# An encoder layer on one core: split halves of W_in kept in DRAM, all conv taps on VectorE, the sample gather issued ahead of the weight subtracts

## The reference

```
h    = rmsnorm(x) * g
q, k, v, cv, cg = split(h @ w_in)            # w_in: 1024 x 1792
A    = attention(rope(rms(q)), rope(rms(k)), v)            # 8 heads on 2, width 64
C    = silu(layernorm(depthwise_conv31(cv * sigmoid(cg)) + b))
x    = x + concat(rms(A), rms(C)) @ w_out
h    = rmsnorm(x);  aff = softmax(h @ w_router)
for each of 16 experts: the top 128 tokens (prompt) and top 64 (sample) by aff:
    y[rows] += gate * (silu(h[rows] @ w_gate) * (h[rows] @ w_up)) @ w_down
```

## Time and profile before

| | |
|---|---|
| median of three runs | 2681.26 us |
| the profiled execution, its own time | 2678.6 us |
| its span, first to last instruction | 2676.7 us |
| busy in the span: TensorE, VectorE, ScalarE, GpSimd | 2555.7, 1852.6, 1393.3, 385.6 us |
| DMA | 477.37 MB, mean 178 GB/s |
| projection of the prompt, of the sample | to 197, to 277 us |
| turning of q and k, attention | 282 to 314, to 628 us |
| output projection and choice, experts | to 876, to 2677 us |

### The profile page before, as it was taken

How to read it: one execution, slowest core, us unless ns; L and a number is a source line. 1 busy time by engine, 2 the same in 40 slices (tenths; PEclk the granted TensorE clock), 3 DMA queues, 4 the chain that set the end, 5 groups by cost and what they waited for, 6 DMA issues and landing times.

```text
span 2676.7 us, 40151 instructions
## 1 busy us (share of the span) xinstructions
PE 2555.7 (95%) x15982; PEld 2349.6 (88%) x15982; DVE 1852.6 (69%) x2177; ACT 1393.3 (52%) x1687; POOL 385.6 (14%) x329
## 2 busy tenths in 40 slices
PE   8989799996995999999999999999999999999997
PEld 8878689985884989999899998999989999899996
DVE  6788899985348567666676666766667666676674
ACT  4233556667222556556565564655656556465563
POOL 3635890000001001001010010100101001010010
PEclk9999999998997999999999999999999999999999
DMA  4122000002323767777687786777868778677773
GB/s 155 44 65 82 1 1 1 1 1 104 111 95 127 233 227 248 225 254 247 223 255 232 242 252 229 248 226 251 249 223 256 231 241 254 229 248 224 244 243 111
DMA packets 348093, 477.37 MB, mean 178 GB/s; under 512 B 10000, under 2 KB 301200, under 8 KB 347792
## 3 DMA queue, kind: packets, MB, share of 16 engines
q1 hardware_dynamic: 340880, 449.74, 51.6%
q0 software_dynamic: 7040, 25.17, 3.8%
HBM read 449.71 MB, written 25.17 MB: 177 GB/s over the span
## 4 chain that ended last, share of the span: by engine, by line
PE 89%; DVE 5%; ACT 3%; issue 1%; POOL 1%; DMA 1%; SPq 0%; ACTq 0%; POOLq 0%; DVEq 0%
PE psum L1592 30%; PE psum L1594 14%; PE psum L1325 8%; PE psum L1326 8%; PE psum L1327 8%; PE psum L1461 5%; PE psum L1614 4%; PE psum L1615 4%; PE psum L1448 2%; PE psum L1436 2%; DVE conv L893 1%; ACT probs L666 1%; PE psum L1577 0%; PE psum L1527 0%; DVE wi_lo L920 0%
## 5 line engine op out<-in xcount | busy, mean ns | idle before, releaser
L1232 DVE TENSOR_TENSOR w_lo<-raw,w_hi 128x2048 fp32r<-128x2048 f32 x384 | 880.0, 2292 | 494.9 <-ACT w_hi L775 493.0
L1592 PE MATMUL psum<-xgT,w_hi 128*128 128x384 f32 x4096 | 1169.0, 360 | 2.4 <-issue 2.4
L1594 PE MATMUL psum<-xgT,w_lo 128*128 128x192 f32 x4096 | 1026.6, 251 | 0.0
L775 ACT CAST w_hi<-raw 128x2048 fp32r<-128x2048 f32 x384 | 733.7, 1911 | 333.0 <-PE psum L1615 333.0
L1594 PEld LDWEIGHTS psum<-xgT,w_lo 128*128 128x128 f32 x4096 | 784.0, 191 | 0.6
L1592 PEld LDWEIGHTS psum<-xgT,w_hi 128*128 128x128 f32 x4096 | 770.5, 188 | 3.5 <-issue 2.8
L549 POOL DMA_INDIRECT out_dram<-o_p,put_p x16 | 25.7, 1605 | 1542.6 <-ACT o_s L822 1471.7
L893 DVE SCALAR_TENSOR_TENSOR conv<-conv,colp 128x1024 f32<-128x1024 f32 (+1 forms) x210 | 236.4, 1126 | 4.0
L1325 PE MATMUL psum<-w_hi,hid_st 128*128 128x512 f32 x512 | 212.9, 416 | 0.0
L1326 PE MATMUL psum<-w_lo,hid_st 128*128 128x512 f32 x512 | 202.5, 396 | 0.0
L1327 PE MATMUL psum<-w_hi,hid_st 128*128 128x512 f32 x512 | 202.4, 395 | 0.0
(11 more groups left out here) (216 smaller groups left out, 3531.8 us busy)
## 6 DMA issues: line engine op xcount, KB each, us to landing
raw<-in_w_gate_dram SPq DMA_DIRECT2D x128, 1024.0 KB, 5.3
raw<-in_w_up_dram SPq DMA_DIRECT2D x128, 1024.0 KB
raw<-in_w_down_dram SPq DMA_DIRECT2D x128, 1024.0 KB, 4.9
wi_raw<-in_w_in_dram SPq DMA_DIRECT2D x56, 256.0 KB, 3.8
out_dram<-x SPq DMA_DIRECT2D x12, 512.0 KB, 2.6
h_rows<-h SPq DMA_DIRECT2D x12, 512.0 KB, 2.9
wo_raw<-in_w_out_dram SPq DMA_DIRECT2D x8, 512.0 KB, 7.3
xres<-in_x_prompt_dram SPq DMA_DIRECT2D x8, 512.0 KB, 4.1
```

The source lines that it names most:

```text
L775: act.copy(w_hi[:, j % SPLIT_SLOTS, :], raw[:, j % RAW_SLOTS, :]).then_inc(e_hi, 1)
L1232: dve.tensor_tensor(w_lo[:, j % SPLIT_SLOTS, :], raw[:, j % RAW_SLOTS, :], w_hi[:, j % SPLIT_SLOTS, :].bitcast(F32), ALU.subtract).then_in ...
L1592: pe.matmul(bank[:, 0:2 * CAP], w_hi[:, slot, w0:w0 + P], xgT[:, half, k, :], start=(k == 0), stop=False, skip_group_check=True)
L1594: last = pe.matmul(bank[:, 0:CAP], w_lo[:, slot, w0:w0 + P], xgT[:, half, k, 0:CAP], start=False, stop=(k == KD - 1), skip_group_check=True)
```

## The change

*W_in's halves.* After each prompt chunk's split, SP writes the halves to a DRAM buffer `wi_kept` (4 writes of 512 KB per chunk, `keep_wi`). For the sample it loads both halves of a chunk whole, two loads of 1 MB (`load_kept`), as soon as TensorE has multiplied the chunk two before. No raw load, cast or subtract remains for the sample; TensorE waits on the load. ScalarE's cast into a slot waits until the slot's earlier halves are written out.

*Conv taps.* The taps of the sample's block 0 join `TAPS` on VectorE; GpSimd has none. Gated blocks of the sample run 6, token steps of its token chunks 0 and 1 run 2. The conv transposes of prompt tiles wait for the prompt's taps alone, and up to 14 units of the sample may still run one tap each.

*The sample gather.* GpSimd waits for two row arrays in place of three, issues, does a small copy, and signals `asked`. VectorE does the prompt's low half first, waits for `asked`, subtracts chunks 0 and 1, then the sample's low half, then chunk 2 onward.

```diff
+    wi_kept = nc.dram_tensor("wi_kept", [CHUNKS, 2, P, KD * CCOLS], F32).ap()
...
-        TAPS = [(0, c, k) for c in range(NC_CONV) for k in range(CONV_K)] + [(1, c, k) for c in (1, 2, 3) for k in range(CONV_K)]
-        POOL_TAPS = [(1, 0, k) for k in range(CONV_K)]
+        TAPS = [(0, c, k) for c in range(NC_CONV) for k in range(CONV_K)] + [(1, c, k) for c in range(NC_CONV) for k in range(CONV_K)]
+        PROMPT_TAPS = NC_CONV * CONV_K
...
+            def keep_wi(place, halves=(0, 1)):
+                for hf in halves:
+                    ks = slice(hf * KD // 2, (hf + 1) * KD // 2)
+                    sp.wait_ge(wi_l, 2 * place + hf + 1)
+                    for x, half in enumerate((wi_hi, wi_lo)):
+                        sp.dma_start(wi_kept[place, x].rearrange("p (k c) -> p k c", k=KD)[:, ks, :], half[:, place % 2, ks, :].bitcast(F32)
+                                     ).then_inc(kept[place % 2], 16)
+            def load_kept(place):
+                n = CHUNKS + place
+                if place < 2:
+                    sp.wait_ge(kept[0], 64 * (3 + place))
+                    sp.wait_ge(kept[1], 64 * 3)
+                wi_multiplied(sp, n - 2)
+                for x, half in enumerate((wi_hi, wi_lo)):
+                    sp.dma_start(half[:, n % 2, :, :].bitcast(F32), wi_kept[place, x].rearrange("p (k c) -> p k c", k=KD)
+                                 ).then_inc(wi_back[n % 2], 16)
...
             for c in range(1, CHUNKS):
-                load_wi(0, c)
+                load_wi(c)
+                keep_wi(c - 1)
             load_x(ROT_TILES)
             load_x(ROT_TILES + 1)
-            load_wi(1, 0)
+            keep_wi(CHUNKS - 1)
+            load_kept(0)
             for t in range(ROT_TILES + 2, TILES):
                 load_x(t)
             for c in range(1, CHUNKS):
-                load_wi(1, c)
+                load_kept(c)
...
-            pool.wait_ge(sample_rows, 3)
+            pool.wait_ge(sample_rows, 2)
             y_stored(pool)
             pool.sem_inc(dma_turn, 1)
             pool.indirect_dma_start(xg_s[:, :], None, h_rows, bass.IndirectOffsetOnAxis(ap=rows_sg[:, 0:1], axis=0)
                                     ).then_inc(gathered_s, 16)
+            pool.tensor_copy(cur_sg[:, :], rows_sg[:, 0:1]).then_inc(asked, 1)
+            pool.wait_ge(asked, 1)
+            pool.wait_ge(sample_rows, 3)
...
                 if n >= 2:
                     wi_multiplied(act, n - 2)
+                    act.wait_ge(kept[n % 2], 64 * (n // 2))
...
-                    if place + 1 < CHUNKS:
-                        split_wi(g, place + 1)
+                    if g == 0 and place + 1 < CHUNKS:
+                        split_wi(place + 1)
...
-                            if (g, c) == (0, 2) and t == nt - 1:
-                                split_wi(1, 0)
...
-                    conv_run(6 if g == 0 else 4)
+                    conv_run(6)
...
-                    conv_run(1)
+                    conv_run(1 if g == 0 or c == 2 else 2)
...
                     conv_run(3 - (u % 4 == 0) if sample_next else 2 - u % 2)
+                elif u < PROMPT_UNITS + 2 * ROT_TILES - 2:
+                    conv_run(1)
                 else:
                     conv_run(len(TAPS))
...
-            for j in range(SPLIT_SLOTS):
+            dve.wait_ge(xg_ph, 1)
+            prompt_low(0)
+            dve.wait_ge(asked, 1)
+            for j in range(2):
                 step(0, j)
-            gathered_low(0, 0)
-            for j in range(SPLIT_SLOTS, TURN):
+            dve.wait_ge(xg_h, 1)
+            sample_low().then_inc(xg_l, 1)
+            for j in range(2, TURN):
                 step(0, j)
...
-                    if ch:
+                    if g == 1:
+                        pe.wait_ge(wi_back[ch % 2], 32 * (place // 2 + 1))
+                    elif ch:
                         pe.wait_ge(wi_l, 2 * ch + 2)
...
-                pe.wait_ge(conv_tap, len(TAPS))
-                pe.wait_ge(pool_tap, len(POOL_TAPS))
+                pe.wait_ge(conv_tap, PROMPT_TAPS if g == 0 else len(TAPS))
```

More of the change, by code:

```diff
@@ L141, in encoder_layer_kernel @@
                 sq = in_region(ra, "sq", [P, CCOLS], F32)
-                tapped = in_region(ra, "tapped", [P, N_SAMPLE], F32)
                 hstat = in_region(ra, "hstat", [P, 2, 3, 4], F32)
@@ L227, in encoder_layer_kernel @@
         wi_h = sem("wi_h"); wi_l = sem("wi_l")
+        kept = [sem(f"kept{i}") for i in range(2)]; wi_back = [sem(f"wi_back{i}") for i in range(2)]
         pr_glu = sem("pr_glu"); glu_sig = sem("glu_sig"); glu_u = sem("glu_u")
@@ L230, in encoder_layer_kernel @@
         t_rstd = sem("t_rstd"); t_norm = sem("t_norm"); rope_a = sem("rope_a"); rope_b = sem("rope_b"); rope_c = sem("rope_c")
-        v_ok = sem("v_ok"); conv_tap = sem("conv_tap"); pool_tap = sem("pool_tap"); pool_mul = sem("pool_mul")
+        v_ok = sem("v_ok"); conv_tap = sem("conv_tap");
         qk_hi = sem("qk_hi"); qk_lo = sem("qk_lo"); qk_T = sem("qk_T"); q_st_ok = sem("q_st_ok"); k_st_ok = sem("k_st_ok")
@@ L252, in encoder_layer_kernel @@
         e_hi = sem("e_hi"); e_lo = sem("e_lo"); e_used = sem("e_used")
-        dma_turn = sem("dma_turn"); cur_ok = sem("cur_ok"); cur_s_ok = sem("cur_s_ok"); put_ok = sem("put_ok"); gathered = sem("gathered"); gathered_s = sem("gathered_s"); xg_T = sem("xg_T"); xg_h = sem("xg_h"); xg_l = sem("xg_l")
+        dma_turn = sem("dma_turn"); cur_ok = sem("cur_ok"); cur_s_ok = sem("cur_s_ok"); asked = sem("asked"); put_ok = sem("put_ok"); gathered = sem("gathered"); gathered_s = sem("gathered_s"); xg_T = sem("xg_T"); xg_h = sem("xg_h"); xg_l = sem("xg_l")
         g_low = sem("g_low"); g_sum = sem("g_sum"); g_act = sem("g_act"); u_low = sem("u_low"); u_sum = sem("u_sum")
@@ L371, in load_x, with load_wi @@
                 sp.dma_start(x_place(t), x_rows(t)).then_inc(x_in[t % ROT_TILES], 16)
-            def load_wi(g, place, halves=(0, 1)):
-                n = CHUNKS * g + place
-                kind, c = ORDER[place]
+            def load_wi(n, halves=(0, 1)):
+                kind, c = ORDER[n]
                 for hf in halves:
@@ L392, in _ @@
             sp.dma_start(colp[:, :], cols).then_inc(consts_in, 16)
-            load_wi(0, 0, (0,))
+            load_wi(0, (0,))
             load_x(2)
-            load_wi(0, 0, (1,))
+            load_wi(0, (1,))
             for t in range(3, ROT_TILES):
@@ L500, in _ @@
                 pool.tensor_tensor(dst, qn[:, n % 2, 0:w], q_turn[:, 0:w], ALU.add).then_inc(rope_c, 1)
[L502 to L513, removed]
             pool.wait_ge(prompt_rows, 1)
@@ L585, in split_x, with split_wi @@
                 act.copy(hT_hi[:, :, i * P:(i + 1) * P], x_transposed(t)).then_inc(hT_h, 1)
-            def split_wi(g, place, halves=(0, 1)):
-                n = CHUNKS * g + place
+            def split_wi(n, halves=(0, 1)):
                 if n >= 2:
                     wi_multiplied(act, n - 2)
+                    act.wait_ge(kept[n % 2], 64 * (n // 2))
                 for hf in halves:
@@ L631, in _ @@
                         if t < 2:
-                            split_wi(0, 0, (t,))
+                            split_wi(0, (t,))
                 for place, (kind, c) in enumerate(ORDER):
-                    if place + 1 < CHUNKS:
-                        split_wi(g, place + 1)
+                    if g == 0 and place + 1 < CHUNKS:
+                        split_wi(place + 1)
                     if kind == "glu":
@@ L887, in conv_run @@
                         dve.wait_ge(glu_u, glu_no[g, c, GROUPS[g][2] // 512 - 1] + 1)
-                        if g == 1:
-                            dve.wait_ge(pool_tap, len(POOL_TAPS))
                         dve.tensor_scalar(out, u, tap, colp[:, COL_BIAS + c:COL_BIAS + c + 1], ALU.mult, ALU.add
@@ L1255, in hid_low, with prompt_low, sample_low @@
                                   ALU.subtract).then_inc(h_lo, 1)
-            def gathered_low(e, half):
[L1258 to L1265, removed]
+            def prompt_low(half):
+                return dve.tensor_tensor(xgT[:, half, :, CAP:CAP + CAP_P], gathered_prompt(),
+                                         xgT[:, half, :, 0:CAP_P].bitcast(F32), ALU.subtract)
+            def sample_low():
+                return dve.tensor_tensor(xgT[:, :, :, CAP + CAP_P:2 * CAP], gathered_sample(),
+                                         xgT[:, :, :, CAP_P:CAP].bitcast(F32), ALU.subtract)
+            def gathered_low(e, half):
+                dve.wait_ge(xg_h, e + 1)
+                last = prompt_low(half)
                 if half == 0:
-                    last = dve.tensor_tensor(xgT[:, :, :, CAP + CAP_P:2 * CAP], gathered_sample(),
-                                             xgT[:, :, :, CAP_P:CAP].bitcast(F32), ALU.subtract)
+                    last = sample_low()
                 last.then_inc(xg_l, 1)
```

## The result

The changed kernel takes 2666.08 us (median of 5 runs, 2664.14 to 2666.31), the kernel before 2681.09 us beside it (5 runs, 2678.01 to 2682.63): a ratio of 0.9943, interval 0.9930 to 0.9956. Forecast were 2668.8 us and a range of 2663 to 2675. Its profiled execution took 2666.08 us with a span of 2664.3 us; against the profiled execution of before (2678.6 and 2676.7) that is 12.5 us, the sum forecast. The medians lie 15.0 us apart because the profiled execution of before is one of the quick ones of its kernel, that of after its median. What makes some executions of before quicker than others is not known.

The account below looks back on a forecast made before the run. TensorE was taken to bound the kernel, with 89% of the chain of waits. Terms −8, −3, +3.5 and −5 sum to −12.5 us, from 2681.26 to 2668.8 us, range 2663 to 2675.

Parts of the forecast that it names:

- the sum forecast: Whole kernel: −8 − 3 + 3.5 − 5 = −12.5 us against the profiled execution.
- prompt attention: Prompt attention's 64 units: without GpSimd's taps all run at 3.61 us, 231 in place of 238.8 us; −8 us.
- The argument from pace and pair of taps: Prompt attention: units 3.95 us beside GpSimd's taps, 3.61 after; two VectorE taps 3.50 against 2.60 us.
- Turning q and k: Stage from 282 to 314 us: small splits that TensorE awaits get shorter without GpSimd's taps; −3 us, bounds 0 and −4.
- the three shorter stretches: Turning of q and k: three stretches of about 0.3 to 0.4 us, counted beside two long ones.
- The split read as running alone: Turning of q and k: a small split taking 0.41 us alone, against 1.48 beside GpSimd's taps.
- Sample projection: Sample's projection: subtracts go, 16 taps come, VectorE ends at 284.0 in place of 280.5; +3.5 us, bounds +0.3 and +9.
- the mean of the window: Sample's projection: each VectorE tap costs 1.40 us, from 27 taps taking 37.82 us.
- The rival of taps contended throughout: Sample's projection: VectorE late, +9 in place of +3.5 us, so 2674.3 us; chance 0.12.
- Queue and kept halves: SP's writes and sample loads: costed at nothing, each later kept pair covered by one TensorE chunk of 11.3 us.
- Start of the experts: Sample gather: issues unheld by VectorE's subtracts, first expert matmul at 871.4 in place of 876.44; −5 us, bounds −6 and −0.2.

Follow-up runs that it names:

- The late pairs: Changed kernel with a 2 MB DRAM-to-DRAM copy queued ahead of each kept pair but the first: 2677.82 us.
- The run with one subtract: Changed kernel with one VectorE subtract of 2048 columns between the prompt's low half and the wait for GpSimd's issue: 2668.93 us.
- the run with copies: Changed kernel with three VectorE copies of 2048 columns between the prompt's low half and the wait for GpSimd's issue: 2666.06 us.
- both edits: Changed kernel with no tap behind the sample's last gated block and attention's row scaling on ScalarE instead of VectorE: 2654.71 us, 0.9912.

## Why the prediction was right

*What bounds it, and prompt attention* (−8): −8.3. Five kernels separate the causes: with GpSimd's taps the 64 units take 238.8 and 238.7 us, without them 230.2, 230.5 and 230.6, whatever else is changed. The argument from pace and pair of taps was the right one. What it took for VectorE's pace is TensorE's as much: VectorE relieved by 14.7 us gave 2.8.

*Turning q and k* (−3): −2.1. The two long splits of 1.48 us became 0.42, which is 2.1 us and the whole of what the stage gained; the three shorter stretches that the term also counted went too, and seem to have been covered, which no run tests. The run without GpSimd's taps gave −1.7. The split read as running alone lay beside a GpSimd multiply (292.86 to 294.47 us), the long one beside an add (291.01 to 292.75); the runs without these taps have the same 0.42.

*Sample projection* (+3.5, an end of VectorE at 284.0): 284.54, and the first q 4.1 us later. Of this 0.8 us came from ahead of the sample's projection: the changed kernel was at 191.67 where before was at 190.89, so TensorE began at 195.64 and not by 195. That isn't shown to be the queue or the kept writes, which were costed at nothing: over all kernels here this point lies between 190.58 and 192.38, with kept halves alone at 190.89, without GpSimd's taps and with no such writes at 192.38. Less this, +3.3. But the stage moves by nearly as much from run to run: without GpSimd's taps the first q came 3.0 us later than before, by the same code. The taps cost what the mean of the window said: in the groups of VectorE from 209 to 284.6 us 42 of them take 59.5 us, 1.42 each, against 1.40, and behind the first gated block VectorE waited for no other, as reckoned. The rival of taps contended throughout did not come.

*Queue and kept halves* (0): no wait; pairs of 1 MB loads land in 4.8 and 6.9 us, inside the 11.3 us. The late pairs show the cover that was reckoned with (11.1 us for a pair that took 14.5), and more only behind a late one.

*Start of the experts* (−5): the issue 0.96 us, landing after 4.3, and the stage 5.7 us shorter; undone it costs 5.2. The forecast took 5.2 us for the landing, as of the prompt's gather; the 0.9 us less is why the stage gained more than reckoned. As to "SBUF — State Buffer", section "Who interferes with whom" of the Trainium skill: by its inferred clause these subtracts would not hold descriptor generation. Here they held the issue, 6.6 us against 0.96 in two kernels that differ in the start of the experts alone. The same section says that the order of issue decides who blocks. The run with one subtract, where GpSimd was first, agrees; the run with copies, where GpSimd was first by as much and the issue took 1.75 us, does not.

*What was not in the sum*: the last sample units gave back about 1 us (9.57 us from the 93rd to the last maximum against 8.50, at a mean granted clock of 0.82 against 1.00), and the expert stage gained 1.0. They cancel, and the second is within what this stage moves: 1798.4 to 1800.6 us in all kernels here but the one with both edits.

So the sum of 12.5 was right by terms of which none is off by more than 1 us. That it met the spans to 0.1 us is luck: the terms missed by 0.3 to 0.9 us to either side. The difference between the medians is 2.5 us more only because of where the profiled execution of before lies among its runs.

## What to carry to other kernels

Before moving work onto an engine, look at what stands behind it there: the taps paid on VectorE only because the splits that TensorE waited for had been taken away, and either edit tried alone would have been judged far from its worth in the pair. Where an engine looks gapless beside another that looks gapless, take some work off one before forecasting from it. And cost a late transfer with its buffers: with two of them a late load shelters the next.

## What the runs showed of the hardware

Taps on GpSimd slow work on VectorE: two VectorE taps took 3.50 us beside GpSimd's and 2.60 alone. Of the small splits, both of 1.48 us began during a GpSimd add; those that began during a multiply took 0.41 or 0.42 us. VectorE subtracts running back to back stretched the issue of an indirect DMA on GpSimd to 6.6 us in place of 0.96, a single one under way to 2.24 us, and one that began after it didn't; a subtract with one input in PSUM (855.64 to 856.85) lay beside the issue without holding it. Three copies of 2048 columns took 1.24 us each where a subtract of as many takes 2.25, and held GpSimd up to their ends too (1.75 and 1.18 us), though the issue had begun first.
